# Two low halves and the negated sinks moved ahead of the rotary steps on VectorE, one cast moved ahead of the last squares between two layers

## What is computed

```
u = rms_norm(x, g_mix_pre)
qa, ka, va, cq, ckv, ga, gb = split(u @ w_in)
qa, ka = rope(qa), rope(ka);          y_a = swa_sink_attention(qa, ka, va, sinks)
qb = rms_norm(cq) @ w_uq;             kv = rms_norm(c_kv) @ w_ukv
k_pe, q_pe = rope(k_pe), rope(q_pe);  y_b = mla_attention(qb, kb, vb)
m = sigmoid(ga + b0) * (y_a @ w_oa) + sigmoid(gb + b1) * (y_b @ w_ob)
x = x + rms_norm(m @ w_out)
x = x + rms_norm(square(relu(rms_norm(x) @ w_mlp_in)) @ w_mlp_out)
```

## Time and profile before

| | |
|---|---|
| median of 3 runs | 766.52 us (766.51 to 766.74) |
| the profiled execution | 765.94 us, of which the span of the profile is 764.2 us |
| PE | busy 750.2 us, 98% of the span |
| PEld | busy 629.3 us, 82% |
| DVE | busy 510.1 us, 67% |
| ACT | busy 419.2 us, 55% |
| POOL | busy 163.2 us, 21% |
| granted clock of PE | 0.998 of full speed |
| DMA queue | 131.64 MB, 51.9% of 16 engines' span |

### The profile page before, as it was taken

One profiled execution on the slowest core, in us unless ns is written; L12 is line 12 of the kernel. 1 busy time (PEld: TensorE's weight loads), 2 busy tenths in 40 slices (PEclk: granted clock), 3 DMA queues, 4 the chain that ended last, 5 costly groups with the idle time before them and its releaser, 6 DMA issues.

```text
span 764.2 us, 10865 instructions
## 1 busy us (share of the span) xinstructions
PE 750.2 (98%) x3970; PEld 629.3 (82%) x3970; DVE 510.1 (67%) x674; ACT 419.2 (55%) x789; POOL 163.2 (21%) x250
## 2 busy tenths in 40 slices
PE   6999999999999999999999999999999999999996
PEld 5978877788798888888888887778887988888885
DVE  5779766667765566656686887675568656565664
ACT  6847775434564444444577686644438444544452
POOL 1966431100131111100125462220002210111110
PEclk9999999999999999999999999999999999999999
DMA  7739533365565555566337483334463656465521
GB/s 255 253 108 298 176 111 111 115 217 169 161 199 187 189 194 171 163 217 208 103 108 253 175 298 111 111 110 166 166 218 113 218 168 220 170 213 170 198 72 55
DMA packets 68619, 132.16 MB, mean 173 GB/s; under 512 B 2874, under 2 KB 10596, under 8 KB 68324
## 3 DMA queue, kind: packets, MB, share of 16 engines
q1 hardware_dynamic: 68308, 131.64, 51.9%
q10 hardware_dynamic: 272, 0.00, 0.0%
HBM read 130.59 MB, written 1.05 MB: 172 GB/s over the span
## 4 chain that ended last, share of the span: by engine, by line
PE 90%; DVE 5%; ACT 2%; issue 1%; DMA 0%; POOL 0%; POOLq 0%; SPq 0%; ACTq 0%; DVEq 0%
PE acc L1335 18%; PE acc L1337 18%; PE acc L1336 18%; PE tp L1620 6%; PE sc L1620 6%; PE tp L1310 4%; PE sc L1417 3%; PE acc L1369 3%; PE tp L1622 3%; PE sc L1622 3%; DVE w_lo L984 2%; DVE x L1149 1%; PE sc L1605 1%; PE sc L1607 1%; PE sc L1606 1%; PE sc L1337 1%
## 5 line engine op out<-in xcount | busy, mean ns | idle before, releaser
L984 DVE TENSOR_TENSOR w_lo<-raw,w_hi 128x1024 fp32r<-128x1024 f32 (+3 forms) x256 | 306.5, 1217 | 152.2 <-ACT w_hi L651 150.8
L651 ACT CAST w_hi<-raw 128x1024 fp32r<-128x1024 f32 (+3 forms) x256 | 250.8, 995 | 186.0 <-PE acc L1337 119.3
L1335 PE MATMUL acc<-w_hi,s_hi 128*128 128x512 f32 (+1 forms) x328 | 127.7, 389 | 0.1
L1337 PE MATMUL acc<-w_hi,s_lo 128*128 128x512 f32 (+1 forms) x328 | 126.6, 386 | 0.0
L1336 PE MATMUL acc<-w_lo,s_hi 128*128 128x512 f32 (+1 forms) x328 | 126.5, 386 | 0.0
L1335 PE MATMUL acc<-w_hi,s_both 128*128 128x512 f32 (+2 forms) x320 | 122.8, 384 | 0.7 <-DVE w_lo L984 0.6
L1336 PE MATMUL acc<-w_lo,s_both 128*128 128x512 f32 (+2 forms) x320 | 118.6, 371 | 0.0
L1337 PE MATMUL acc<-w_hi,s_both 128*128 128x512 f32 (+2 forms) x320 | 118.3, 370 | 0.0
L514 POOL TENSOR_TENSOR tok<-k_b 128x512 f32<-128x512 f32 x32 | 37.0, 1160 | 266.0 <-ACT k_b L747 244.7
L1335 PEld LDWEIGHTS acc<-w_hi,s_hi 128*128 128x128 f32 x328 | 61.6, 188 | 13.1 <-DVE w_lo L984 1.3
L1337 PEld LDWEIGHTS acc<-w_hi,s_lo 128*128 128x128 f32 x328 | 61.6, 188 | 12.4
(11 more groups left out here) (179 smaller groups left out, 1076.3 us busy)
## 6 DMA issues: line engine op xcount, KB each, us to landing
raw<-in_w_mlp_in SPq DMA_DIRECT2D x32, 1024.0 KB, 5.3
raw<-in_w_mlp_out SPq DMA_DIRECT2D x32, 1024.0 KB, 5.0
raw<-in_w_in SPq DMA_DIRECT2D x24, 1024.0 KB, 5.5
raw<-in_w_oa SPq DMA_DIRECT2D x8, 1024.0 KB, 5.0
raw<-in_w_out SPq DMA_DIRECT2D x8, 1024.0 KB, 4.9
raw<-in_w_ob SPq DMA_DIRECT2D x4, 1024.0 KB, 5.0
raw<-in_w_in SPq DMA_DIRECT2D x3, 768.0 KB, 4.6
raw<-in_w_in SPq DMA_DIRECT2D x4, 576.0 KB, 6.4
```

Source lines behind the costliest of these rows:

```text
L651: s.copy(split_view(w_hi, p), raw_view(p)).then_inc(hi_ready, 1)
L984: v.tensor_tensor(split_view(w_lo, p), raw_view(p), split_view(w_hi, p).bitcast(F32), ALU.subtract)\
L1335: mm(banks[t][:, 0:N], h[:, kk, tk], wh[:, k, :], start=(start and k == 0), stop=False)
L1337: ins = mm(banks[t][:, 0:N], low[:, kk, tk], wh[:, k, :], start=False, stop=(stop and k == b - a - 1))
```

## The change

On DVE, in each layer:

- the two instructions that write `neg_sink` stand ahead of the low half of the turned `ckv` instead of behind it;
- the low half of piece 19 is made ahead of the first rope instead of inside it, and that of piece 20 inside it instead of behind it;
- the low half of piece 23 is made ahead of the second rope instead of inside it, and that of piece 24 inside it instead of behind it.

On ACT, once, between the layers: the cast of the next layer's piece 2 stands ahead of the squares of the second half of tile 1 instead of behind them and behind the split of the turned `x`.

```diff
@@ ACT, first_of_next
                         turned_hi(after, ("x", 0, 0))
+                        hi(after, 2)
@@ DVE
                 lo(pos, 18)
-                turned(pos, ("ckv",))
-
                 dve.wait_ge(sinks_loaded, pos.count(16, 16))
                 for x_ in range(2):
...
+                turned(pos, ("ckv",))
+
                 dve.wait_ge(tables_ready, 1)
                 for c, p in ((0, 18), (1, 22)):
-                    lo(pos, p)
+                    lo(pos, p + 1)
                     dve.wait_ge(proj_out, pos.count(14, 2 * PROJ[f"q{c}"] + 1))
                     rope(v, steps, probs[:, 0, :], q_of_group(0, c).rearrange("p h (c d) -> p h c d", c=2), AG, AD // 2, 0, 1,
-                         between=lambda: lo(pos, p + 1)).then_inc(roped, 1)
+                         between=lambda: lo(pos, p + 2)).then_inc(roped, 1)
```

## The result

| | before | after |
|---|---|---|
| median | 766.52 us (765.86 to 767.13, 17 runs) | 767.9 us (767.12 to 768.64, 17 runs) |
| ratio | | 1.0019, 95% interval 1.0012 to 1.0025 |
| span of the profiled execution | 764.2 us | 765.7 us |
| PE busy | 750.2 us | 750.0 us |
| DVE busy | 510.1 us | 510.1 us |

The change makes the kernel 1.4 us slower, 0.19%: clear of zero by its interval, and its median just under the 0.2% that I had called a difference. Forecast was 767.5 us, in a range of 766.3 to 768.7, and most of the chance (0.74) on less than 0.2%.

The account below looks back on a forecast made before the run. PE, busy 98% of the span, was taken as the bound. -0.79 + 0.9 + 0.9 + 0.0 = +1.0 us on the profiled 765.94 gave 766.95; with the median's 0.58 on top, 767.5 us, range 766.3 to 768.7.

Parts of the forecast that it names:

- Part 1: Low half of piece 19 ahead of the first rope: PE's stop before piece 19 in layer 0 goes, -0.79 us; layer 1 nothing.
- Part 2: Low half of piece 23 ahead of the second rope waits for ACT's cast: +0.9 us (0.7 to 1.3) in each layer.
- those 1.3 us: Second rope in layer 1: DVE's line 364 ends at 438.94 instead of 437.64, 1.30 us later, and PE waits there.
- Part 3: Earlier cast of piece 2 where the layers meet: 0.0 us (0 to +0.15), as the wait chain does not go through it.
- The rule of the Trainium skill: Second rope: VectorE and GpSimd lock each other out for whole instructions; in full, +2.4 us in sum, 768.9, chance 0.06.
- the second rope is hidden: Rival: the later second rope costs PE nothing, only the gain at piece 19 is left, 765.7 us; chance 0.12.
- PE's idle time where the layers meet goes: Rival: second rope hidden, and PE's waits between layers go too (0.6 us cast, 0.2 low half), 764.9 us; chance 0.04.
- The side over 0.2% slower: Rival: DVE's turns with POOL at the second rope cost full instructions, 768.9 us, or high ends, 768.5; chance 0.22.

## Why the prediction was right

**Part 1** named the right stop and the right cause. It was 0.14 us short in size: the sum took the distance of two starts (0.79 us lost), but the first matmul behind a stop also takes longer to the next start. In the kernel before it was 0.34 us (53.63 to 53.97) in place of 0.23, which is 0.11 of the 0.14; the other 0.03 is a drift between the two traces ahead of piece 19. The whole step measures -0.93, in the changed kernel and with that move alone.

**Part 2** named the gate (the cast of 23 behind ACT's two copies), what stands behind it and who waits. Experiments bear them out: the loss is there with this move alone, it goes when the cast comes first, and it goes when POOL stays away. The turns with POOL were carried over from the rows of before almost to the hundredth. With the clock of layer 1 shifted by 0.32 us (ACT's cast of 23 starts at 432.60 after and at 432.28 before), the forecast 438.94 for the end of line 364 becomes 439.26, and it measured 439.28. The term that was mis-sized is the last one: how much of those 1.3 us is left behind piece 26. I took 0.9, near the lower end, with the reason that the copies ran beside POOL without loss. The low half of 25 had to take a turn with POOL's next rope (439.32, 1.12 us), so that of 26 was late as well and PE stopped at 442.94 too. 1.08 and 1.10 were measured, inside the bounds of 0.7 to 1.3.

**Part 3** was right in its sum, nothing, and in its reason, that DVE's queue ends that stretch. It named the wrong low half. I had expected PE to wait longer for the low half of piece 3. That wait is as before (0.25 us), and the new stop is at the low half of piece 2, the first of these two rows:

```profile
390.67 0.62 PE L1370 MATMUL acc<-w_lo,s_both 128*128 128x384 f32 x2 [0.32 <-DVE w_lo L985]
391.54 0.62 PE L1370 MATMUL acc<-w_lo,s_both 128*128 128x384 f32 x2 [0.25 <-DVE w_lo L985]
```

PE was 0.77 us ahead for a moment, by the cast (from +0.36 to -0.41). It gave back 0.42 at this stop, and the rest in small steps before it, just behind the end of DVE's split (388.30) and of the update of x (389.63).

**The rule of the Trainium skill** (SBUF — State Buffer, section "SBUF: two separate sides", on the exclusive lock between VectorE and GpSimd) agrees with the traces as to the lock. With POOL away, the same instructions take 0.68 and 0.69 us that took 1.77 and 1.67 beside it. Read so that a blocked instruction takes its whole time after the release, it would have given +2.4 us, and 1.4 were measured. The rows again show less than a whole instruction behind the release. This is POOL's row after in layer 1:

```profile
434.22 1.48 POOL L360 TENSOR_TENSOR tok<-tok,cost 128x512 f32<-128x512 f32 x1
```

It ends at 435.70, and DVE's line 359 ended at 434.48 + 1.77 = 436.25, 0.55 us behind it and not 0.69.

**The rivals.** That the second rope is hidden fell with PE's new stops. That PE's idle time where the layers meet goes fell with the cast alone. The side over 0.2% slower (0.22) was missed by 0.15 us (1.53 against 1.38), which is less than the width of the interval, so that it was missed is partly luck. Of the 0.4 us between forecast and result, the two second ropes give 0.38 and part 1 takes 0.14 back; the rest is within what the medians scatter.

## What to carry to other kernels

An instruction moved up in a queue brings its own wait with it: before moving it, look when its input is made and what will now stand behind that wait. Here the input came 0.95 us later than the start of the step that it was put ahead of, and that step was needed just in time. Where two engines take turns, as DVE and POOL do here, the time of a row is that of the turn, not of the work (1.77 us beside POOL, 0.68 without it). Moving the other engine's work away can then shorten a stretch a good deal: one wait on POOL took 2.9 us out of DVE's. What that is worth is another matter, since the work moved away is needed too: PE gained no more by it than by moving the cast, and only both together kept the half microsecond a layer beyond that.

## What the runs showed that I had not expected

- The program's start differs from one execution to the next by more than most effects here. The turn of the second tile of x on PE starts at 13.09 in one trace and at 14.55 in another, though nothing ahead of it was changed. The larger part of that is in the twelve matmuls of 384 columns just ahead of it: they take 2.55 us in the first trace (from 10.70) and 3.46 us in one that turns at 14.54 (from 11.24), some starting 0.17 us apart and the others 0.32. The granted clock reads 1.00 in these stretches, so what sets the spacing stays open. The distance of matmuls inside the trace tells apart what the medians of 11 runs do not.
- A time saved on DVE can be taken up by its turn with POOL: the low half of piece 19 started 1.5 us sooner in the kernel with the sinks moved and ended only 0.6 us sooner, of which 0.17 is that trace's earlier start.
- The first matmul behind a stop is 0.11 us longer to the next start (0.34 in place of 0.23), and the few behind it cost some hundredths more.
